# Shifting six weight tiles and one activation tile by 8 to 136 bytes in on-chip memory

## The reference, cut to what matters

```python
z = h @ w_in[l]                                   # 1024 x 2560
y = concatenate([head_rmsnorm(y_a), head_rmsnorm(y_b)]) @ w_out[l]
q = xb @ w_q
act = gelu(einsum('phkd,pd->phk', expert_u[idx], xb))     # chosen experts
return einsum('phk,phkd->pd', g * act, expert_v[idx])
...
proj = xn @ w_in_2
merged = gate_a * (ya @ w_branch_a) + gate_b * (yb @ w_branch_b)
h = h + merged @ w_out_2
return (silu(xn @ w_gate) * (xn @ w_up)) @ w_down
```

## Time and profile before

| what | value |
|---|---|
| median of 2 runs | 2518.4 us (2516.34 to 2520.46) |
| the profiled execution | 2516.58 us, span 2515.2 us |
| PE busy | 2456.2 us, 98% of the span |
| PEld busy | 2023.0 us, 80% |
| DVE busy | 1577.4 us, 63% |
| ACT busy | 884.8 us, 35% |
| POOL busy | 761.3 us, 30% |
| mean granted TensorE clock | 0.99 |

### The profile page before, as it was taken

One profiled execution on the slowest core, in us unless ns is written; L12 is line 12 of the kernel. 1 busy time (PEld: TensorE's weight loads), 2 busy tenths in 40 slices (PEclk: granted clock), 3 DMA queues, 4 the chain that ended last, 5 costly groups with the idle time before them and its releaser, 6 DMA issues.

```text
span 2515.2 us, 29977 instructions
## 1 busy us (share of the span) xinstructions
PE 2456.2 (98%) x11288; PEld 2023.0 (80%) x11288; DVE 1577.4 (63%) x3102; ACT 884.8 (35%) x1362; POOL 761.3 (30%) x473
## 2 busy tenths in 40 slices
PE   6999999999999999999999999999999989999998
PEld 3778878888778888888888888888888778888887
DVE  6675698679996883445665555554676547444333
ACT  4433432333334333233333333334445543322221
POOL 1434227776877670000000000004333332111100
PEclk9989999999999999999999999999999999999999
DMA  7656666666676775346464555534232343332332
GB/s 273 211 182 210 176 177 144 140 143 176 143 185 151 193 176 201 113 159 226 167 227 166 209 184 185 208 101 130 85 115 88 98 163 96 97 99 95 92 105 80
DMA packets 189190, 388.02 MB, mean 154 GB/s; under 512 B 47148, under 2 KB 114860, under 8 KB 181296
## 3 DMA queue, kind: packets, MB, share of 16 engines
q1 hardware_dynamic: 147928, 324.88, 40.4%
q0 software_dynamic: 41120, 61.23, 10.0%
HBM read 312.72 MB, written 70.98 MB: 153 GB/s over the span
## 4 chain that ended last, share of the span: by engine, by line
PE 68%; DVE 3%; ACT 1%; DMA 1%; issue 0%; ACTq 0%; POOLq 0%
PE bank L526 19%; PE bank L530 19%; PE bank L527 19%; PE bank_stat L879 1%; PE bank_stat L880 1%; PE bank_stat L884 1%; DVE hot_weight L1931 1%; PE bank L762 1%; PE bank L911 1%; PE bank L909 1%; PE bank L924 1%; PE bank L677 1%; DVE weights_lo L1572 1%; PE bank_stat L552 0%; PE bank L543 0%; PE bank L544 0%
## 5 line engine op out<-in xcount | busy, mean ns | idle before, releaser
L526 PE MATMUL bank<-h_lo,weights_hi 128*128 128x512 f32 x2204 | 865.9, 393 | 8.3 <-DVE gates L2200 3.8
L527 PE MATMUL bank<-h_hi,weights_hi 128*128 128x512 f32 x2204 | 862.6, 391 | 0.0
L1063 ACT ACTIVATE weights_hi<-weights_raw 128x1024 fp32r<-128x1024 f32 (+1 forms) x411 | 432.8, 1053 | 418.2 <-PE bank L530 313.9
L530 PE MATMUL bank<-h_hi,weights_lo 128*128 128x512 f32 x2204 | 547.3, 389 | 2.6 <-DVE weights_lo L1572 2.6
L1572 DVE TENSOR_TENSOR weights_lo<-weights_raw,weights_hi 128x1024 fp32r<-128x1024 f32 x351 | 443.0, 1263 | 103.7 <-ACT weights_hi L1063 89.0
L2376 POOL DMA_INDIRECT expert_coefs<-share,place_at x256 | 442.0, 1727 | 194.8 <-issue 95.1
L526 PEld LDWEIGHTS bank<-h_lo,weights_hi 128*128 128x128 f32 x2204 | 416.5, 189 | 95.6 <-DVE gates L2200 3.9
L530 PEld LDWEIGHTS bank<-h_hi,weights_lo 128*128 128x128 f32 x2204 | 413.6, 188 | 90.4 <-DVE weights_lo L1572 4.5
L527 PEld LDWEIGHTS bank<-h_hi,weights_hi 128*128 128x128 f32 x2204 | 416.4, 189 | 85.0 <-issue 0.2
L1789 DVE SCALAR_TENSOR_TENSOR residual<-bank,ada,residual 128x512 f32<-128x512 f32 x135 | 101.5, 752 | 313.8 <-PE bank L530 313.8
L1274 ACT ACTIVATE hidden<-bank 128x512 f32<-128x512 f32 x128 | 76.6, 598 | 455.6 <-PE bank L530 447.9
(11 more groups left out here) (405 smaller groups left out, 2894.1 us busy)
## 6 DMA issues: line engine op xcount, KB each, us to landing
weights_raw<-in_expert_u SPq DMA_DIRECT2D x128, 512.0 KB
weights_raw<-in_expert_v SPq DMA_DIRECT2D x128, 512.0 KB
weight<-expert_coefs POOLq DMA_DIRECT2D x16, 2048.0 KB, 8.5
hidden_store<-hidden SPq DMA_DIRECT2D x26, 1024.0 KB
hidden<-hidden_store POOLq DMA_DIRECT2D x13, 2048.0 KB, 14.5
ada_raw<-in_w_ada SPq DMA_DIRECT2D x34, 512.0 KB, 6.5
expert_coefs<-zeros SPq DMA_DIRECT2D x32, 512.0 KB, 6.3
expert_coefs<-stage SPq DMA_DIRECT2D x16, 1024.0 KB, 6.1
```

The lines of the kernel that those rows point to most:

```text
L526: M.matmul(bank[:], hi[:, c:c + P], m_lo[k], start=start and i == 0, stop=False)
L527: M.matmul(bank[:], hi[:, c:c + P], m_hi[k], start=False, stop=False)
L530: ins = M.matmul(bank[:], lo[:, c:c + P], m_hi[k], start=False, stop=stop and i == len(tiles) - 1)
L1063: S.activation(w_hi[n % SPLIT][:, 0:w], w_raw[n % RAW][:, 0:w], ACT.Copy).then_inc(*hi_done.inc(n))
```

## The change

The tiles of the weights and `h_lo` get other places. `h_lo` lies 8 bytes further up in a tile that is 32 bytes larger. The six weight tiles begin 0, 16, 48 bytes (hi) and 80, 128, 136 bytes (lo) further up by 512 than `h_hi`. Two spacers, 480 and 352 bytes, make all tiles behind them keep their rests by 512; those of the weights' raw tiles, `mixed`, `lru`, `merged` and `ffn` are the old ones. The distances between stationary and moving tile change from 0 (`h`, `mixed`, `ffn`), 256 (`lru`) and 192 (`merged`) accordingly. Since 1,024 bytes more are taken up, `place_at` and `share` now lie in the two halves of `square`. No instruction, wait, transfer or order on any engine is added, taken away or moved.

```diff
-        h_lo = sb("h_lo", [P, KD, T], F32R)
+        h_lo_room = sb("h_lo", [P, KD * T + 8], F32R)
+        h_lo = h_lo_room[:, 2:2 + KD * T].rearrange("p (k t) -> p k t", k=KD)
+        sb("h_lo_spacer", [P, 120])
...
-        w_hi = [sb(f"weights_hi{i}", [P, BLOCK], F32R) for i in range(SPLIT)]
-        w_lo = [sb(f"weights_lo{i}", [P, BLOCK], F32R) for i in range(SPLIT)]
+        weight_tiles = []
+        for name, before, shift in (("weights_hi0", 0, 0), ("weights_hi1", 0, 4), ("weights_hi2", 0, 4),
+                                    ("weights_lo0", 0, 4), ("weights_lo1", 0, 8), ("weights_lo2", 0, 2)):
+            tile = sb(name, [P, BLOCK + (8 if shift else 0)], F32R)
+            weight_tiles.append(tile[:, shift:shift + BLOCK])
+        sb("weights_spacer", [P, 88])
+        w_hi, w_lo = weight_tiles[0:3], weight_tiles[3:6]
...
-        place_at = sb("place_at", [P, SCATTERED, HEADS * TOPK], U32, route)
-        share = sb("share", [P, SCATTERED, HEADS * TOPK], F32, route)
+        place_at = square[:, 0, 0:SCATTERED * HEADS * TOPK].rearrange("p (b c) -> p b c", b=SCATTERED).bitcast(U32)
+        share = square[:, 1, 0:SCATTERED * HEADS * TOPK].rearrange("p (b c) -> p b c", b=SCATTERED)
```

## The result

| what | before | after |
|---|---|---|
| median | 2518.4 us | 2565.45 us (2562.46 to 2568.44, 2 runs) |
| ratio | | 1.0187, 95% interval 1.0124 to 1.0249 |
| profiled execution | 2516.58 us, span 2515.2 us | 2562.46 us, span 2561.1 us |

The point forecast of 2540 us was 25 us too low. The time lies in the range of 2435 to 2575 us, and the forecast had the sign and the mechanism. It had them with some luck: the text held the sign nearly open, its own estimate of 17 to 32 us more missed the measured 46 to 47, and the result lies just inside the 2566 us up to which it had stretched its likeliest case. The middle of the result is just under the 2% that the text on record took as its bound, with an interval that reaches over it.

The account below looks back on a forecast made before the run. The prediction took PE's pace of 512-column float32r matmuls to bound the kernel. Some 7,900 matmuls x 3.1 ns = 24 us, all other parts 0 or left out, on 2516.6 us gave 2540 us, range 2435 to 2575 us.

Parts of the forecast that it names:

- the sign: Whole kernel: slower, 2516.6 + 24 = 2540 us, 1.0% more; the text called the sign nearly open.
- the mechanism: float32r matmuls on PE: pace depends on how load and stream lie in time and address; shifted tiles lose the 32-clock state.
- its likeliest case: Whole kernel: the forecast's own case, 2533 to 2549 us and somewhat around it, up to 2566, chance 0.36.
- the 2%: Whole kernel: what a measurement can tell from no change, 50 us; slower by more is rival 3, faster rival 2.
- What bounds the kernel: PE, busy 98% of the span: time is the number of 512-column float32r matmuls times their pace, 226.67 ns.
- The writers: ACT and DVE writing weight tiles at shifted places: cost 0, as nothing shows that writing depends on the place.
- Rival 1: Shifted matmuls: the old state holds, or one near it, 2495 to 2520 us; chance 0.27.
- rival 2: Shifted matmuls: load and stream come free of each other, pace below 220.3 ns, full effect 2430 us; chance 0.22.
- The mis-sized term: Matmuls at new distances: 3.1 ns more each, the middle of +2.2 and +4.1; 24 us in all.
- The count: Matmuls that get another distance: 6219 of `h` and gates, 1703 of `mixed` and `ffn`, together some 7,900.
- Rival 3: Shifted matmuls: blocks stay at a steady bad pace of 233 to 236 ns, over 2% slower, up to 2590 us; chance 0.15.
- wandering: Blocks on shifted tiles: with six distances and two moving tiles, none finds the 32-clock state for long; 3.1 ns more.

Follow-up runs that it names:

- the room alone: Changed kernel with `h_lo` and all six weight tiles back at distance 0, keeping spacers and `place_at` and `share` in `square`: 2517.59 us, ratio 0.9995.
- the two maps: Two kernels without the computation, only 512-column float32r matmuls at varied places, 81 groups of 96 and 512 groups of 40: none below 544 clocks.
- the map of distances: Own kernel without the computation: 81 groups of 96 float32r matmuls, load 0 to 512 bytes from the stream; 544.0 to 564 clocks.
- the map of pairs: The map of distances with another loop: 512 groups of 40 matmuls, `h_lo` moved 0 to 224 bytes, load 0 to 248; 556.8 clocks on the mean.
- run with `h_lo` alone: Changed kernel with all six weight tiles back at distance 0, `h_lo` still 8 bytes up: 2546.3 us, ratio 1.0106.
- The last kernel: Kernel with all hi tiles at 120 and lo tiles at 376 bytes, attention tiles moved 192 bytes so `merged` has these distances: 2512.95 us, ratio 0.9969.

## Why the forecast was right, and what was off

**What bounds the kernel**: right. PE's busy time grew by 51.3 us and the span by 45.9; no other engine's moved by more than 1.2 us. The writers, `place_at`, `share` and the room cost 0, as put (ratio 0.9995 with the room alone; GpSimd's subtractions take 2462 ns against 2464). That a writer's time does not depend on the place held for this change only: at 120 and 376 bytes GpSimd's was 17% shorter.

**The mechanism**: right in its main point. The pace is a steady state that some relations of the two streams find and others don't, and the change leaves it. Rival 1 (the old state holds) and rival 2 (free streams) fell: all 593 groups of the two maps are at 544 clocks or above. The ground of rival 2, plain float32 with 2.3 ns over, did not carry to float32r; bfloat16 at full rate has as little over (6 clocks), though with a shorter load, so the half rate, my reason against it, isn't needed for that. The earlier trace rows are eleven records, two to a matmul, so the half rate was that of a record. By the rule of the Trainium skill ("TensorE: Matmul & The Clock Gate", Part 2), that the load takes no read bandwidth from the stream, the place of a load should not matter to the pace. bfloat16 and plain float32 agree with that at six distances each; float32r doesn't, its pace goes from 544 to 576 clocks with the place. Whether bandwidth is what it loses there no run shows.

**The mis-sized term** is the new excess: I took 3.1 ns, the middle between the steady row at distance 192 (+2.2) and the mean behind a wait (+4.1). It is 5.8 ns on the mean of all matmuls in the long stretch and about 6.2 on those that changed. Neither row was the right kind. The earlier trace rows was one steady state of several at that distance: the map of distances has 192 bytes at 233.4 ns, the map of pairs at 228.8. And paces behind a wait are those of a run that is on its way down to 544, so their mean is below that of relations that never get there: 556.8 clocks over 512 pairs, 5.3 ns above 544.

**The count** was a little low, too. I kept the matmuls on `weights_hi0` with `h_hi` at their old pace because their own distance stays 0. The run with `h_lo` alone shows that they are lost with their partner (235.0 ns for the pair). On `mixed`, where both partners stay, the count was nearly right: 228.5 ns, the 1.8 over 226.7 being the first four and the last matmul of each block; those between have 226.7. The corrected count is 6996 + 1703 = 8699. Summed start by start at full clock, the matmuls on `h`, `mixed` and `ffn` take 42.3, 9.0 and 2.3 us more, 53.6 together, or 6.2 ns for each of the 8699; the others add 1. Of this 5.4 us came back as shorter waits of PE, 2.9 of them in the routing stretch, which my sum had as nothing, and up to 7 us through the higher mean clock of this execution. That leaves 42 to 49 us; the measured difference is 45.9.

**Rival 3**, slower by over 2%, was nearly met: its point was a pace of 233 ns, the change has 232.5. Its picture of blocks that stay at one bad end was nearer than mine of wandering: 560 clocks is where more than half of the distances settle, and in the real kernel the blocks of one moving tile and one buffer mostly repeat their pace within 0.3 ns.

## What to carry to other kernels

Where TensorE runs float32r matmuls back to back, read the pace, not the busy share, and compare it with the columns in clocks; 544 for 512 is as low as any of 593 groups came, so for a kernel at a steady 226.7 ns these runs know no better place. The last kernel's 0.3% came from stretches that had not settled, from `merged` and from something that is open. Keep tiles of one role at the same rest by 256 bytes as their partners, and after any edit that moves tiles look at the pace again: in this kernel an arbitrary placement cost 2%. A row taken from a settling stretch is no estimate for a state that doesn't settle.

## What the runs showed of the hardware

- float32r, 512 columns, a load beside each: 544 clocks at best, 548 to 576 elsewhere. It hangs on the distance by 256 bytes and also on the common place: distance 0 has 233.5 ns with both operands 8 bytes further up and 239.2 with both 4 bytes up.
- One distance can have two steady paces in one execution (233.3 and 226.5 ns at 16 bytes); runs of that kernel differ by 35 us, perhaps for it.
- Steady paces often go in steps: 504, 510 and 512 columns take 544 clocks (508 takes 546.5), 496 and 500 take 536. 448 and 464 do not fall on a step.
- bfloat16 takes 518.0 clocks, and plain float32 1030.0 for each of the two records of a matmul, at each of six distances.
- A load of 32 columns instead of 128 does not make the float32r pace shorter (231.7 ns against 226.8).
- GpSimd's subtraction of a 128x1024 block took 2464 ns with the tiles in their old places and 2056 to 2061 with hi tiles at 120 and lo tiles at 376 bytes.

What it is in the reads or the timing of float32r that makes the steps stays open. The runs speak against the amount that the load reads, and against other engines' work, since the maps have none beside them. No run streams float32r without a load beside it, so whether the 32 clocks over at the best places have to do with the load at all is untested.
